# A decoder trunk on one core: the projection's scaling moved behind the matmuls, loads and waits split by use, attention's output copy placed ahead of the running sum

## What is computed

```python
p = rms_norm(x, g_attn) @ w_in              # 1024 -> 2840 columns
q, k = rope(rms_norm(q, g_q)), rope(rms_norm(k, g_k))
kc, vc = gelu(blocks(k_cmp) @ w1) @ w2      # compressed blocks, prompt and cache
# group A: three softmax branches a head: compressed, selected, window; merged by gates
# group B, stick-breaking, a head:
z = q @ k.T * HEAD_DIM ** -0.5
log_1m = where(mask, log_sigmoid(-z), 0)
a = where(mask, exp(log_sigmoid(z) + suffix_sum(log_1m)), 0)
o = a @ v
h = x + mix @ w_out;  y = h + (silu(g) * u) @ w_down
```

## Time and profile before

| | us |
|---|---|
| median of 3 runs | 2978.65 (2967.43 to 2986.84) |
| the profiled execution, its own time | 2984.64 |
| span of the profile | 2983.0 |
| PE busy in the span | 2451.3 (82%) |
| DVE, ACT, POOL busy | 1210.5, 753.9, 795.2 |

### The profile page before, as it was taken

One profiled execution on the slowest core, in us unless ns is written; L12 is line 12 of the kernel. 1 busy time (PEld: TensorE's weight loads), 2 busy tenths in 40 slices (PEclk: granted clock), 3 DMA queues, 4 the chain that ended last, 5 costly groups with the idle time before them and its releaser, 6 DMA issues. The chain is left out here.

```text
span 2983.0 us, 42604 instructions
## 1 busy us (share of the span) xinstructions
PE 2451.3 (82%) x12910; PEld 1832.7 (61%) x12910; DVE 1210.5 (41%) x1923; ACT 753.9 (25%) x1347; POOL 795.2 (27%) x817
## 2 busy tenths in 40 slices
PE   2988986589991788888888884548989999999999
PEld 0344443445540566666666662334489999999999
DVE  0587777333320444444444552224321111124443
ACT  0110100233320444443434440001121111123332
POOL 0788888212201232222323221412100000000000
PEclk9999998699995877876877886779989999999999
DMA  5467766898837543442443323332121111112200
GB/s 196 145 192 223 231 216 215 165 128 109 108 37 151 145 121 85 122 112 78 117 114 95 98 89 102 70 109 93 56 86 46 46 46 49 46 51 93 68 30 24
DMA packets 268753, 320.85 MB, mean 108 GB/s; under 512 B 60565, under 2 KB 175031, under 8 KB 268173
## 3 DMA queue, kind: packets, MB, share of 16 engines
q1 hardware_dynamic: 207502, 246.94, 30.4%
q0 software_dynamic: 17600, 47.50, 8.8%
q10 hardware_dynamic: 43472, 24.26, 2.7%
HBM read 284.79 MB, written 38.53 MB: 108 GB/s over the span
## 5 line engine op out<-in xcount | busy, mean ns | idle before, releaser
L393 PE MATMUL pp<-w_in_sb,xT_sb 128*128 128x512 f32 (+3 forms) x864 | 365.4, 586 | 0.3 <-DVE xT_sb L419 0.3
L236 POOL TENSOR_TENSOR key_products<-key_pages,sb_q_rows 128x512 f32<-128x512 f32 x256 | 337.8, 1343 | 78.8 <-DMA key_pages<-in_cache_sb_kv 52.5
L1885 PE MATMUL pg<-h_turned_hi,w_gu_hi 128*128 128x344 f32 x1056 | 338.3, 320 | 9.8 <-DVE h_turned_lo L1933 9.8
L1887 PE MATMUL pg<-h_turned_hi,w_gu_lo 128*128 128x344 f32 x1056 | 338.3, 320 | 0.0
L1886 PE MATMUL pg<-h_turned_lo,w_gu_hi 128*128 128x344 f32 x1056 | 338.1, 320 | 0.0
L393 PEld LDWEIGHTS pp<-w_in_sb,xT_sb 128*128 128x128 f32 (+1 forms) x864 | 163.6, 192 | 193.5 <-issue 182.2
L651 PE MATMUL ph_c<-rows_turned,w_cmp 128*128 128x510 f32 (+1 forms) x576 | 252.6, 566 | 15.5 <-ACT rows_turned L675 12.1
L2011 PE MATMUL py<-w_down_hi,act_hi 128*128 128x256 f32 x792 | 225.7, 285 | 9.9 <-DVE w_down_lo L2058 9.9
L2012 PE MATMUL py<-w_down_lo,act_hi 128*128 128x256 f32 x792 | 225.0, 284 | 0.0
L2013 PE MATMUL py<-w_down_hi,act_lo 128*128 128x256 f32 x792 | 225.0, 284 | 0.0
L1928 DVE TENSOR_TENSOR w_gu_lo<-late,w_gu_hi 128x512 fp32r<-128x512 f32 x88 | 60.9, 692 | 402.0 <-ACT w_gu_hi L1898 402.0
(11 more groups left out here) (265 smaller groups left out, 4274.1 us busy)
## 6 DMA issues: line engine op xcount, KB each, us to landing
key_pages<-in_cache_sb_kv SPq DMA_DIRECT2D x256, 256.0 KB, 3.0
late<-in_cache_sb_kv SPq DMA_DIRECT2D x256, 256.0 KB, 3.0
late<-in_w_gate_up SPq DMA_DIRECT2D x88, 256.0 KB, 2.9
late<-in_cache_nsa_kv SPq DMA_DIRECT2D x128, 128.0 KB, 6.6
late<-in_cache_nsa_kv POOLq DMA_DIRECT2D x128, 128.0 KB, 5.8
late<-in_w_down SPq DMA_DIRECT2D x4, 2816.0 KB, 10.6
w_in_sb<-in_w_in SPq DMA_DIRECT2D x5, 2048.0 KB, 14.7
scratch_T_hi<-turned_hi ACTq DMA_DIRECT2D x8, 896.0 KB
```

The costliest lines, as they stand in the source:

```text
L236: eng.tensor_tensor(prod[:, m % PR], kr[:, m % KR], qb[:, b % 2], ALU.mult).then_inc(multiplied, 1)
L393: mm = eng.matmul(pp[0:R, m % 4, 0:b - a], xT[:, u, k, 0:R], w[:, k, a:b], start=(k == 0), stop=(k == KT - 1))
L1885: eng.matmul(pg[:, e, c, 0:CW], w_hi[:, h, j, :], hT_hi[:, k, cols], start=k == 0, stop=False)
L1887: mm = eng.matmul(pg[:, e, c, 0:CW], w_lo[:, h, j, :], hT_hi[:, k, cols], start=False, stop=k == KT - 1)
```

## The change

In `project` DVE no longer scales the rows: PE transposes them raw, and ACT multiplies by the reciprocal root while it copies a piece from PSUM (`scale=`). POOL's `join_rows` becomes two ACT copies in `store_rows`. `rotate` does in 6 products what took 10 (the rotary table now holds cos, cos, -sin, sin over 64 columns), and waits for the 16 small loads only where it first uses them. SP's loads stand in another order, the key ring has 6 buffers, and `PAGES` differs. ACT issues `store_turned` after the squares of the heads. In `compress` parking is split after batch 6. In `attend` the waits for loads are split by what needs them, the keys load from ACT's queue, z has two buffers, and DVE's `scan` and ACT's last exponential of a tile stand one step later.

```diff
-        PAGES = [(0, 0, 8, 8)] + [(8, 6, 8, 8)] * TILES
+        PAGES = [(0, 0, 0, 8)] + [(8, 7, 8, 8)] * TILES
...
                 load(0)
+                eng.dma_start(gat[:, :], ...).then_inc(gat_loaded, 16)
-                for c, (a, b) in list(enumerate(COLS))[1:]:
+                for c, (a, b) in enumerate(COLS):
                     eng.dma_start(w[:, :, a:b], wv[:, :, a:b]).then_inc(w_loaded[c], 16)
+                    if c == 2:
+                        load(1)
                 eng.dma_start(table[:, :], ...).then_inc(table_loaded, 16)
-                load(1)
...
@@ ACT, store_rows(n)
+                    eng.wait_ge(roped, n + 1)
...
+                    eng.activation(kv[:, :, 0, :], rv, ACT.Copy)
+                    eng.activation(kv[:, :, 1, :], pv[:, :, 1, :], ACT.Copy).then_inc(kv_copied, 1)
...
-                        eng.activation(pj[0:R, u, a:b], pp[...], ACT.Copy).then_inc(proj_saved, 1)
+                        eng.activation(pj[0:R, u, a:b], pp[...], ACT.Copy, scale=ss[0:R, u, 1:2]).then_inc(proj_saved, 1)
...
-                    if n >= 1:
-                        store_turned(n - 1)
                     eng.drain()
...
                     eng.activation(g["gates"][...], pj[0:R, u, GATE0:GATE0 + 24], ACT.Sigmoid)
+                    if n >= 1:
+                        store_turned(n - 1)
@@ PE
-                        if c == 3 and n >= 1:
-                            head_transposes(n - 1, (0, 1))
-                        if c == 4 and n >= 1:
-                            head_transposes(n - 1, (2, 3))
                         if c == 4 and n + 1 < NTILE:
                             x_transposes(n + 1)
+                        if c == 4 and n >= 1:
+                            head_transposes(n - 1, (0, 1))
+                        if c == 5 and n >= 1:
+                            head_transposes(n - 1, (2, 3))
@@ DVE
-                eng.wait_ge(c_loaded, 16 * 17)
...
-                norm_x(0)
+                eng.wait_ge(gat_loaded, 16)
                 save_xT(0)
                 for n in range(NTILE):
+                    for k in (0, 1):
+                        for m in pages(n, k):
+                            reduce(m)
                     if n + 1 < NTILE:
-                        norm_x(n + 1)
-                    for m in pages(n, 0):
-                        reduce(m)
+                        save_xT(n + 1)
                     if n >= 1:
                         save_turned(n - 1, (0, 1))
-                    for m in pages(n, 1):
+                    for m in pages(n, 2):
                         reduce(m)
                     if n >= 1:
                         save_turned(n - 1, (2, 3))
...
@@ compress, SP
-                eng.wait_ge(keys_saved, NB + 1)
...
+                for b0, b1 in ((0, 6), (6, NB)):
+                    eng.wait_ge(keys_saved, b1 + 1)
+                    xs = slice(KVH * b0, KVH * b1)
+                    eng.dma_start(io["kcT_s"][:, KVH * b0 * NCS:KVH * b1 * NCS], ...).then_inc(parked, 16)
+                    eng.wait_ge(values_saved, b1 + 1)
+                    eng.dma_start(vc_s[:, 0, xs], vc[:, 0, xs]).then_inc(parked, 16)
+                    eng.dma_start(vc_s[0:P - 1, 1, xs], vc[0:P - 1, 1, xs]).then_inc(parked, 16)
@@ attend, PE
-                eng.wait_ge(const_loaded, 16 * 9)
-                eng.wait_ge(keys_loaded, 16 * 4)
                 eng.wait_ge(consts_set, 1)
...
                     if s % H == 0:
-                        eng.wait_ge(head_loaded[u], N * 160 + 160)
-                        eng.wait_ge(values_loaded[u], N * 16 + 16)
+                        eng.wait_ge(sb_loaded[u], N * 96 + 96)
+                    if s % H == 1:
+                        eng.wait_ge(nsa_loaded[u], N * 64 + 64)
+                    if zero(N) and s == 2:
+                        eng.wait_ge(keys_loaded, 64)
...
+                    if zero(N) and m == 1:
+                        eng.wait_ge(vx_loaded, 64)
...
                     if s == 3:
+                        if zero(h):
+                            eng.wait_ge(dec_loaded, 32)
@@ attend, ACT
                     if s % 4 == 0:
+                        if not (zero(N) and s < 4):
+                            stick_exp(N, s)
+                            eng.wait_ge(scan_done, k)
                         eng.wait_ge(z_copied, k + 1)
...
-                    else:
-                        eng.wait_ge(logw_ready, k + 1)
...
-                        eng.activation(prs[:, 0:w], dd[:, 0:w], ACT.Exp).then_inc(stick_done, 1)
@@ attend, DVE
-                        if s % 4 == 2:
-                            scan(N, s)
                         if not (zero(N) and s < 3):
                             out(N, s - 3)
+                        if s % 4 == 3:
+                            scan(N, s)
```

More of the change, by code:

```diff
@@ L267, in _ @@
                         row_norm(n + 1)
-                    for i, m in enumerate(pages(n, 0)):
-                        if i == 4:
-                            join_rows(n - 1)
-                        multiply(m)
-                    for k in (1, 2):
+                    for k in (0, 1, 2):
                         for m in pages(n, k):
@@ L278, in _ @@
                         multiply(m)
-                join_rows(TILES)
             @block.scalar
@@ L452, in rotate @@
                     eng.drain()
[L453 to L454 removed]
+                    eng.tensor_tensor(ro[0:R], ra[0:R], rb[0:R], ALU.add).then_inc(roped, 1)
                 def save_turned(n, groups):
@@ L485, in _ @@
                         save_turned(n - 1, (2, 3))
-                    if n + 1 < NTILE:
-                        save_xT(n + 1)
-                    for m in pages(n, 2):
-                        reduce(m)
                     rotate(n)
@@ L789, in attend @@
         vr = late[:, 0:4096].rearrange("p (r n) -> p r n", r=RING)
-        zs, lg, rl, dd = (late[:, 4096 + i * SEQ:4096 + (i + 1) * SEQ] for i in range(4))
+        lg, rl, dd = (late[:, 5120 + i * SEQ:5120 + (i + 1) * SEQ] for i in range(3))
+        zs = [late[:, 4096:5120], late[:, 10240:11264]]
         PER = 16 * NPAGE // RING
@@ L1076, in _ @@
             def _(eng):
+                turned_rows = {part: io[part].rearrange("(h d) t -> d h t", d=HD) for part in ("T_hi", "T_lo")}
+                for i, t in enumerate((T_KS, T_KW)):
+                    eng.dma_start(kT[0:HD, i].bitcast(F32), turned_rows["T_hi"][:, t:t + 2, :]).then_inc(keys_loaded, 16)
+                    eng.dma_start(kT[HD:P, i].bitcast(F32), turned_rows["T_lo"][:, t:t + 2, :]).then_inc(keys_loaded, 16)
                 eng.preload_act_table_set("natural_log_exp_and_others")
@@ L1087, in exps, with stick_exp @@
                     eng.activation(pr[:, s % 2, 0:w], S[:, s % 2, 0:w], ACT.Exp, bias=nm[:, s:s + 1]).then_inc(exp_done, 1)
+                def stick_exp(N, s):
+                    w, k = width(FRONT[(s - 4) % U]), N * NSTICK + s // 4 - 1
+                    eng.wait_ge(logw_ready, k + 1)
+                    if not (zero(N) and s < 8):
+                        m = back_of(s - 8)
+                        eng.wait_ge(turned, N * G + (m // U) * G + G0[m % U + 1])
+                    eng.activation(prs[:, 0:w], dd[:, 0:w], ACT.Exp).then_inc(stick_done, 1)
                 def stick(N, s):
@@ L1092, in stick @@
                     if s % 4 == 0:
+                        if not (zero(N) and s < 4):
+                            stick_exp(N, s)
+                            eng.wait_ge(scan_done, k)
                         eng.wait_ge(z_copied, k + 1)
-                        if not (zero(N) and s < 4):
-                            eng.wait_ge(scan_done, k)
-                        eng.activation(lg[:, 0:w], zs[:, 0:w], ACT.Abs)
+                        eng.activation(lg[:, 0:w], zs[s // 4 % 2][:, 0:w], ACT.Abs)
                     elif s % 4 == 1:
@@ L1145, in tail @@
                         save_groups(eng, 4, s - 2, 1)
+                    if s == 0:
+                        stick_exp(4, 0)
                     if s == 2:
@@ L1170, in stat @@
                         return
-                    if not (zero(N) and s < 4):
-                        eng.wait_ge(logw_ready, N * NSTICK + s // 4)
-                    eng.tensor_copy(zs[:, 0:w], z).then_inc(z_copied, 1)
+                    if not (zero(N) and s < 8):
+                        eng.wait_ge(logw_ready, N * NSTICK + s // 4 - 1)
+                    eng.tensor_copy(zs[s // 4 % 2][:, 0:w], z).then_inc(z_copied, 1)
                 def scan(N, s):
```

134 lines of the change are left out of this document (57 added, 77 removed).

## The result

| | us |
|---|---|
| before, median of 4 runs | 2980.93 (2967.43 to 2986.84) |
| the change, median of 4 runs | 2831.21 (2823.41 to 2835.46) |
| ratio, 95% interval | 0.950 (0.946 to 0.954) |
| profiled execution, before and after | 2984.64 and 2823.41 |
| span, before and after | 2983.0 and 2821.5 |

What follows compares the result with a forecast made beforehand. It gave each stage its own bound: projection work handed round with no engine full, attention's PE waiting on the output copy at clock 0.80. Terms -60 - 15 - 5 - 85 = -165 gave about 2815 us against the median, range 2715 to 2910.

Steps and rivals of the forecast that it cites:

- Start of the projection: Projection: PE starts at 12.5 us, POOL at 57, last pieces of tiles 0 and 1 at 54 and 106; gains 43 us.
- A tile: Projection: a tile's period falls to 49 us (47 to 52), gaining 2 us in each of seven tiles.
- the term of 60: Projection, start, tiles and tail together: compress starts 60 us earlier (45 to 75).
- four products lie ready in their buffers: Projection tile, DVE's 15 page sums: four products ready, eleven more at POOL's 1.344 us each, 14.8 us.
- the ring of 6 buffers: Projection: the key ring's 6 buffers cost nothing, since PE, DVE and POOL set the period.
- Parking and start of attention: Splitting parking shortens its tail by 15 us; separate load counters bring attention's start 5 us earlier.
- The loop: Attention's loop: gains 85 us (0 to 190), 50 from waits and 35 from clock.
- The copy moves ahead of the running sum: Attention's loop: PE's 100.8 us of waits for the output copy go; about half return as later sums, gaining 50.
- The first rival, a wait that only moves: Attention's loop: PE waits as long for the stick exponential instead, loop gains nothing; 2900 us, chance 0.22.
- Its bounds for the loss of before: Attention's loop: PE's time lost to the lowered clock before the change, 97 to 163 us.
- The closed loop: Attention: the chain from running sum back to the next sum lengthens and binds, 3 us a tile; 3090 us, chance 0.04.
- The clock that recovers: Attention runs near 2.4 GHz once the copy waits go, loop gains 180 us; about 2720 us, chance 0.17.

Runs made afterwards that it cites:

- root_later: The change with POOL's root of the head sums behind four of a projection tile's last eight products instead of two; 2814.46 us, ratio 0.946.
- rows_126: The change with each parking transfer of 127 rows made two, of 126 rows and 1 row; 2821.58 us, ratio 0.949.
- sum_at_2: The change with DVE's running sum put back one step, into the output copy's step and behind that copy; 2901.44 us, ratio 0.973.
- fill_4: The change with four unread 512-column matmuls more per attention tile, ahead of PE's wait for the stick weights; 2773.45 us, ratio 0.931.

## Why the prediction was right, and where it was not

The sum came within 4 us of the profiled difference, -165 for -161.2, and that is luck in part: the projection gave 13 us less than its term and the loop 9.5 more.

**Start of the projection.** Right: PE, the last pieces of tiles 0 and 1 and POOL's first product came within 2.5 us of the forecast. (For tile 0 the terms as written, 12.5, six pieces of 6.9 and 2, add up to 55.9 and not to 54; the piece of 280 columns took 3.8 us.)

**A tile.** Mis-sized: 50.5 us, not 49, which is some 10 of the 13 us missing from the term of 60; against before's 51.1 a tile gains 0.6 us and not 2. The rotation was right: it ends 381.67 - 362.19 = 19.5 us after the last piece, forecast 19.8. The term that failed is "four products lie ready in their buffers, eleven more come at POOL's 1.344 us, 14.8 us". Only one product lies ready: in the sixth tile every sum but the first waits for POOL, and the 15 take 399.48 - 381.67 = 17.8 us. So the second transposes come 40.0 us after the last piece, not 38.8, though the copies ahead of them took less than was put down. Behind this, "the ring of 6 buffers, since PE, DVE and POOL set the period" left out which of the three: POOL is busy 318.00 / 7 = 45.4 us of 50.5 and idle mostly at one wait of its own order, the root's, as `root_later` showed.

**Parking and start of attention.** Right, -16.4 and -6.2 for -15 and -5; the reason for the first was tested in `rows_126`, that for the second by no run.

**The loop.** The size was right (-94.5 for -85; 45 of waits for 50, 49.5 of clock for 35). The step that failed is its reason: "The copy moves ahead of the running sum, so the 100.8 us go. What is late next is the sum." With the copy moved alone the waits for the softmax weights grow by 108.5 - 24.9 = 83.6 us, and the loop gains 11. The prediction read PE's waits and not those of DVE, where the sum's own wait for the Ln, 101.8 us, was as large and delayed whatever stood behind it. It counted the sum's later step as a cost, yet it is that step that takes the wait off: with the sum put back, `sum_at_2`, the loop is 820 us again. So the loop's right size came by another way than the one described. The first rival, a wait that only moves, would have been right for the copy alone, though at another place.

**The clock.** The prediction could not say which waits come before a fall: in before it was the wait for `o_raw` at 26 of 37. `fill_4` shows what the falls behind the stick weights cost in the change: filling those waits freed 97.7 us of PE's time. Its bounds for the loss of before, 97 to 163 us, were of the right size: the same work took 693.39 us there and 546.2 in `fill_4`, 147 less.

**The rivals.** The closed loop didn't bind. The clock that recovers came only in part in the change (0.85) and nearly whole in `fill_4` (0.97).

## What to carry to other kernels

When an instruction of an in-order engine waits long, look for what stands behind it: here, moving one victim ahead handed most of the wait to the next, and moving the waiter to where its input is ready ended it. Where TensorE's granted clock is under 1 in a busy loop, find the waits that come right before the falls; cheap matmuls into unread columns there can be worth more than they cost. A transfer's count of rows is worth a look: 126 + 1 instead of 127 took the tail from 8.9 to 3.1 us.

## What was not expected of the hardware

VectorE and GpSimd slow each other. The same product of 896 columns in `rotate`, beside POOL's products in tile 7 and after POOL's last one (which ends at 476.75) in tile 8:

```profile
428.99 2.15 DVE L426 TENSOR_TENSOR qk_squares<-normed,rot_sb 128x896 f32<-128x896 f32 x1
```

```profile
477.62 1.08 DVE L426 TENSOR_TENSOR qk_squares<-normed,rot_sb 128x896 f32<-128x896 f32 x1
```

POOL's products, six beside DVE's products in a rotation and six beside its page sums and copies:

```profile
368.13 9.01 POOL L235 TENSOR_TENSOR key_products<-key_pages,sb_q_rows 128x512 f32<-128x512 f32 x6
```

```profile
404.44 7.39 POOL L235 TENSOR_TENSOR key_products<-key_pages,sb_q_rows 128x512 f32<-128x512 f32 x6 [0.79 <-DVE z_all L391]
```

DVE's product takes up to twice as long while POOL multiplies (a product of the same size took 1.30 us, between the two, at 380.37 in the sixth tile), and POOL's takes 9.01 / 6 = 1.50 us instead of 7.39 / 6 = 1.23. So a duration of DVE from a stretch with an idle POOL, or the reverse, is no price for the other. And 256 matmuls more made a kernel 2% faster.
